# First and last stage of a three-block network kernel: the order of the loads, and the last columns by pairs

## The chip, the cores and the metric

The kernel runs on one core of a Trainium2 chip. The core has five engines with an instruction stream each: TensorE (matmuls and transposes, results in PSUM), VectorE, ScalarE, GpSimd and SyncE (SP), which only issues DMAs here. They are ordered among each other by semaphores alone. The metric is the device time of one execution in microseconds; lower is better. All data are fp32, and a product is made of three passes on high and low parts.

## What is computed

A sequence of 1024 positions with 1024 features goes through three blocks. Cut to what this change touches, the reference is:

```python
def rmsnorm(x, g):
    y = x * rsqrt(mean(x * x, -1) + EPS)
    return y * g

# first block, start
h = rmsnorm(x, norm_mix_g)
z = h @ w_in                      # the gate's low-rank columns (1536..) are projected first
q, k, v, g, a_f, a_b, su, sv = split(z)
...
# third block, end
pe = p @ w_pp                     # K = 256
gate = sigmoid(rms_norm_3(h, pe_norm_g) @ w_pg)
h = h + gate * pe
return rms_norm_3(h, final_g)
```

Between them lie gated linear attention and a spatial gating unit, an MLP, a state space layer with differential attention, and a convolution beside a gated recurrence.

## The kernel before

The program of every engine is written as functions of its own (`pe_...`, `act_...`, `dve_...`, `pool_...`, `sp_...`), called in program order. A table `at` gives every event a semaphore and a count: `inc` records it and `wait_ge(*at[event])` waits for it. `ended` and `fence` record and await the end of a stage on all semaphores. DMAs of SP rotate over 16 semaphores and those of ScalarE over 8, and `Engine.dma` waits until the earlier DMA on the same semaphore has landed.

Activations stand transposed in `HTh` and `HTl` (high and low part, features on partitions, 8 groups of 128 = k, two halves of 512 positions = th). Weights come in units: up to 8 x 128 rows by 256 columns, loaded by SP into one of three `WR` buffers (`sp_unit`), copied by ScalarE to a rounded high part in one of two `WH` buffers (`act_unit`), subtracted by VectorE to a low part in one of three `WL` buffers (`dve_unit`), and used by TensorE (`pe_unit`, `pe_done`). In the first call `sp_unit` takes units 0 to 2, `act_unit` and `dve_unit` take units 0 and 1; each later call takes one more, so the splits run one unit ahead of TensorE. Unit 0 has 128 columns (512 KB), unit 1 and most others 256 (1 MB); a `w_pp` unit has two groups of 128 rows only (256 KB).

PSUM has eight banks of 128x512: the ring `PD` with four for the projections and the ring `PB` with four (the two halves of the two `PQt` tiles). `take` goes round a ring; some users take fixed banks with `put`: squares go to `PB` banks 0 and 1, the late transposes to 2 and 3, and attention writes to `PQt` directly.

**Setup.** GpSimd makes the identity and zeroes four tiles `PRc`. SP loads four groups of small vectors (`COLS`; 10, 1, 1 and 9 parts) as rows into them, and four lambda vectors. TensorE transposes each tile, VectorE copies it to `PC` (so `pc(name, i)` is a column with one value per partition) and makes the lambda values, with one exponential by ScalarE between. Then all engines pass a fence.

**First norm and projection.** SP loads x in 8 tiles (`sp_load_x`). ScalarE squares each with an accumulator (`act_squares`, L484), VectorE and GpSimd make 1/sqrt per half (L492, L497), VectorE scales (L562), TensorE transposes (`pe_to_ht`, L359), ScalarE and VectorE write high and low part with the norm's gain (L523, L531). `act_norm` and `dve_norm` call `between` (the unit split, L311 and L320) after the first half's splits. TensorE's order is: transposes of half 0, projection `fm` of unit 0 for half 0 (L211, 24 matmuls), the late transposes of half 1 in two `PB` banks, `fm` for half 1, then the filling rounds.

**The end.** `pe_final` goes over four groups of 256 output columns (n) and in each over four pairs of tiles (t4): gate products `pg` from a `w_pg` unit, then `pp` products from a `w_pp` unit; a pair takes 48 matmuls for `pg` and 12 for `pp`. ScalarE writes the sigmoid (L3768), VectorE multiplies it by `pp` (L3782), GpSimd adds it to `X3` (L3795). After n = 3 ScalarE squares the eight tiles (L484), the powers are made per half (L492, L497), VectorE scales by half (L1583), and SP stores each tile.

Of the kernel before, what the change touches and what calls it, by code (L numbers as in the profile page):

```python
# [17 lines left out]
NT = 8  # L18
# [209 lines left out]
def program(nc, A, out, ctx):  # L228
# [74 lines left out]
    def act_unit(e):  # L303
        n = turn("act")
        for i in ([0, 1] if n == 0 else [n + 1]):
            if i < len(units):
                e.wait_ge(*at["w_landed", i])
                if i >= 2:
                    e.wait_ge(*at["w_used", i - 2])
                z = units[i][0]  # L310
                e.activation(WH[i % 2][:, 0:z], WR[i % 3][:, 0:z], ACT.Copy).then_inc(*at.inc("wh", "wh", i))  # L311

    def dve_unit(e):
        n = turn("dve")
        for i in ([0, 1] if n == 0 else [n + 1]):
            if i < len(units):
                z = units[i][0]
                e.wait_ge(*at["w_landed", i])
                e.wait_ge(*at["wh", i])
                e.tensor_tensor(WL[i % 3][:, 0:z], WR[i % 3][:, 0:z], WH[i % 2][:, 0:z].bitcast(F32),  # L320
                                SUB).then_inc(*at.inc("wl", "wl", i))

    def sp_unit(e):
        n = turn("sp")
        for i in ([0, 1, 2] if n == 0 else [n + 2]):
            if i < len(units):
                if i >= 3:
                    e.wait_ge(*at["w_used", i - 3])
                for dst, src in units[i][1]:
                    e.i.dma_start(dst, src).then_inc(*at.landed(f"wr{i % 3}", "w_landed", i))  # L330
# [69 lines left out]

    ph = ExitStack()
    PRc = [sbt(ph, [128, 128]) for _ in COLS]
# [4 lines left out]
    def pool_setup(e):  # L407
        e.memset(ident[:, :], 0.0).then_inc(*at.inc("pool", "z"))
# [6 lines left out]
        for i in range(4):  # L415
            e.memset(PRc[i][:, :], 0.0).then_inc(*at.inc("pool", "PR0", i))

    def sp_setup(e):
        for i, parts in enumerate(COLS):
            e.wait_ge(*at["PR0", i])  # L420
            for j, (name, ap) in enumerate(parts):
                r = col[name] - i * 128
                e.dma(PRc[i][r:r + ap.shape[0], :], ap, "col_in", i, j)
        for i, n in enumerate(("lambda_q1_2", "lambda_k1_2", "lambda_q2_2", "lambda_k2_2")):
            e.dma(lv[:, i, :], A[n].partition_broadcast(128).rearrange("p a d -> p (a d)"), "lv", i)

    def pe_setup(e):
        e.wait_ge(*at["const"])
        for i, parts in enumerate(COLS):
            b = e.take(PB, "col", i)  # L430
            for j in range(len(parts)):
                e.wait_ge(*at["col_in", i, j])
            e.transpose(b[:, 0:128], PRc[i][:, :], ident[:, :]).then_inc(*at.inc("pe", "col", i))

    def dve_setup(e):
        for i in range(4):
            e.wait_ge(*at["col", i])
            e.tensor_copy(PC[:, i * 128:i * 128 + 128], PB.of("col", i)[:, 0:128]).then_inc(
                *at.inc("dve", "PC", i, free=("col", i)))
        for i in range(2):  # L440
# [5 lines left out]
            e.tensor_reduce(lam[:, i:i + 1], lv[:, 4, :], AX.X, ADD).then_inc(*at.inc("dve", "lvs", i))  # L446
        e.wait_ge(*at["lam_exp"])
# [3 lines left out]
        e.wait_ge(*at["PC", 0])  # L451
        e.tensor_scalar(pc("subln"), pc("subln"), 1.0 - LAM_INIT, None, MUL).then_inc(*at.inc("dve", "subln"))

    def act_setup(e):
        e.wait_ge(*at["lvs", 1])
        e.activation(lam[:, 0:2], lam[:, 0:2], ACT.Exp).then_inc(*at.inc("act", "lam_exp"))
# [6 lines left out]
    def sp_load_x(e, X, src, *event):  # L463
        v = src.rearrange("(t p) d -> p t d", p=128)
        for tt in range(NT):
# [90 lines left out]
    def dve_norm(e, X, XN, v, ready, gname, vacant=(), between=lambda e: None):  # L556
# [9 lines left out]
        for tt in range(4):  # L566
            scaled(tt)
# [3433 lines left out]
```

## Time and profile before

| | |
|---|---|
| median of three timed runs | 3949.09 us (3943.42, 3949.09, 3951.37) |
| the profiled execution | 3947.51 us |
| its span | 3945.6 us |
| TensorE busy | 3713.4 us, 94% |
| VectorE / ScalarE / GpSimd busy | 2167.5 / 1653.1 / 520.3 us |
| TensorE's mean granted clock | 0.973 of 2.4 GHz |

Engines run beside each other, so busy times don't add up to the span. What counts is the time in which TensorE has nothing to do, and why. Times in the rows are microseconds from the start of the span; PEclk is the share of 2.4 GHz that was granted.

### The profile page before, as it was taken

How to read it: one execution, taken by the hardware profiler on the slowest of the kernel's cores; microseconds unless marked ns; L12 is line 12 of the kernel's file. 1: busy time of each engine (PE TensorE's matmuls, PEld its weight loads, DVE VectorE, ACT ScalarE, POOL GpSimd, SP SyncE). 2: the span in 40 equal slices, each digit the busy share in tenths (PEclk: the TensorE clock that was granted, in tenths of full speed). 3: DMA queues.
4: the chain of work that ended last, by engine and by line, in shares of the span. 5: the costliest groups of instructions: out<-in, count | busy, mean ns of one | idle time of the engine just before them, and what ended most of it. 6: DMA issues, size and time to landing. Idle time of an engine off the chain costs nothing.

```text
span 3945.6 us, 48879 instructions
## 1 busy us (share of the span) xinstructions
PE 3713.4 (94%) x20470; PEld 3102.4 (79%) x20470; DVE 2167.5 (55%) x2859; ACT 1653.1 (42%) x2267; POOL 520.3 (13%) x437
## 2 busy tenths in 40 slices
PE   6979999999999899989999998989999999989998
PEld 5758988877787677777777777978877778778998
DVE  4343344334446566645665655358888877853332
ACT  4322232121113555646776674144555545542132
POOL 0000010010001243510000000012222221210001
PEclk9989999999999899999999999999999999999999
DMA  3101211111111111010111114121111111143111
GB/s 95 33 11 50 75 59 54 43 51 46 43 54 55 43 33 43 12 49 24 33 35 27 35 48 163 49 75 43 43 43 38 49 48 38 38 183 132 44 44 59
DMA packets 196399, 211.32 MB, mean 54 GB/s; under 512 B 7943, under 2 KB 171732, under 8 KB 196180
## 3 DMA queue, kind: packets, MB, share of 16 engines
q1 hardware_dynamic: 191572, 191.42, 15.3%
q10 hardware_dynamic: 4608, 16.78, 1.1%
q8 instruction: 162, 2.65, 0.3%
q14 instruction: 57, 0.47, 0.0%
HBM read 174.62 MB, written 33.55 MB: 53 GB/s over the span
## 4 chain that ended last, share of the span: by engine, by line
PE 78%; DVE 9%; ACT 6%; issue 4%; DMA 1%; POOL 1%; SPq 0%; DVEq 0%; ACTq 0%; POOLq 0%
PE pd L211 66%; PE pq L211 9%; PE pd L359 2%; PE pq L359 1%; ACT t L311 1%; DVE t L320 1%; DVE t L2989 1%; ACT t L2586 1%; DVE t L3426 1%; ACT t L523 1%; DVE t L2981 0%; DVE t L1923 0%; DVE t L1495 0%; DVE t L3411 0%; DVE t L531 0%
## 5 line engine op out<-in xcount | busy, mean ns | idle before, releaser
L211 PE MATMUL pd<-t 128*128 128x512 f32 (+2 forms) x15920 | 3080.9, 354 | 41.6 <-DVE t L1495 10.1
L211 PEld LDWEIGHTS pd<-t 128*128 128x128 f32 x15920 | 2556.5, 191 | 513.0 <-issue 90.2
L211 PE MATMUL pq<-t 128*128 128x128 f32 (+5 forms) x3222 | 542.8, 331 | 83.6 <-DVE t L3465 21.5
L211 PEld LDWEIGHTS pq<-t 128*128 128x128 f32 (+2 forms) x3222 | 391.6, 182 | 184.4 <-issue 47.3
L311 ACT ACTIVATE t<-t 128x2048 fp32r<-128x2048 f32 (+2 forms) x150 | 244.9, 1633 | 677.9 <-PE pd L211 634.0
L320 DVE TENSOR_TENSOR t<-t 128x2048 fp32r<-128x2048 f32 (+2 forms) x150 | 297.3, 1983 | 287.8 <-ACT t L311 287.4
L1495 DVE TENSOR_TENSOR t<-pd,t 128x512 f32<-128x512 f32 x256 | 171.2, 689 | 115.7 <-PE pd L211 115.7
L1486 DVE TENSOR_TENSOR t<-t 128x512 fp32r<-128x512 f32 x64 | 45.8, 719 | 261.3 <-POOL t L1474 261.3
L3378 POOL TENSOR_TENSOR t<-t 128x512 f32<-128x512 f32 x56 | 89.8, 1603 | 616.8 <-ACT t L3322 608.9
L2989 DVE SCALAR_TENSOR_TENSOR t<-t 128x1024 f32<-128x1024 f32 x120 | 169.6, 1413 | 0.5
L2981 DVE SCALAR_TENSOR_TENSOR t<-t 128x1024 f32<-128x1024 f32 x120 | 166.2, 1385 | 1.7
L2709 DVE COPY t<-pd 128x512 f32<-128x512 f32 x64 | 44.3, 691 | 217.6 <-PE pd L359 217.6
L359 PE MATMUL pd<-t 128*128 128x128 f32 x800 | 119.8, 294 | 42.5 <-DVE t L562 18.6
L359 PEld LDWEIGHTS pd<-t 128*128 128x128 f32 x800 | 101.1, 152 | 65.2 <-issue 20.9
L2586 ACT ACTIVATE t<-t 128x1024 f32<-128x1024 f32 x128 | 145.8, 1142 | 13.8 <-DVE t L2663 13.8
L2658 DVE CUSTOM_DVE_ANT_0 t<-pq,t 128x1024 f32<-128x1024 f32 x128 | 151.2, 1219 | 0.0
L3322 ACT ACTIVATE t<-t 128x1024 f32<-128x1024 f32 x56 | 59.4, 1062 | 215.4 <-DVE t L3413 215.4
L1474 POOL TENSOR_TENSOR t<-t 128x512 f32<-128x512 f32 x64 | 68.2, 1067 | 613.1 <-ACT t L1424 613.1
L1424 ACT ACTIVATE t<-pd 128x512 f32<-128x512 f32 x64 | 38.3, 598 | 244.9 <-PE pd L211 244.9
L3426 DVE COPY_PREDICATED t<-t,pq 128x512 f32<-128x512 int32 x128 | 94.7, 743 | 70.1 <-PE pq L211 69.7
L1591 POOL TENSOR_TENSOR t<-t 128x2 f32<-128x2 f32 x8 | 10.4, 1303 | 917.5 <-DVE t L2826 857.1
L713 DVE TENSOR_TENSOR t<-pd,t 128x512 f32<-128x512 f32 x48 | 33.2, 691 | 176.5 <-PE pd L211 176.5
(295 smaller groups left out, 2830.5 us busy)
## 6 DMA issues: line engine op xcount, KB each, us to landing
t<-in_w_in_dram SPq DMA_DIRECT2D x97, 512.0 KB, 4.3
t<-in_w_mlp_dram SPq DMA_DIRECT2D x32, 1024.0 KB, 5.3
t<-in_w_out_dram SPq DMA_DIRECT2D x20, 1024.0 KB, 5.1
t<-in_w_in_dram SPq DMA_DIRECT2D x16, 1024.0 KB, 5.2
t<-in_x_dram SPq DMA_DIRECT2D x16, 512.0 KB, 6.6
x_scratch<-t SPq DMA_DIRECT2D x16, 512.0 KB, 2.6
ym_scratch<-t SPq DMA_DIRECT2D x16, 512.0 KB, 2.6
t<-x_scratch SPq DMA_DIRECT2D x16, 512.0 KB, 20.0
```

Source lines behind the costliest of these rows:

```text
L211: ins = e.matmul(out, l, r, start=(first and j == 0), stop=(last and j == n - 1), skip_group_check=True)
L311: e.activation(WH[i % 2][:, 0:z], WR[i % 3][:, 0:z], ACT.Copy).then_inc(*at.inc("wh", "wh", i))
L320: e.tensor_tensor(WL[i % 3][:, 0:z], WR[i % 3][:, 0:z], WH[i % 2][:, 0:z].bitcast(F32), SUB).then_inc(*at.inc("wl", "wl", i))
L359: ins = e.transpose(b[:, j * 128:(j + 1) * 128], s, ident[:, :])
L1474: e.tensor_tensor(q[:, :], r[:, :], r[:, :], MUL).then_inc(*at.inc("pool", "q", j, m, th, free=("r", j, m, th)))
L1495: e.tensor_tensor(X1[:, tt, half(nh)], PD.of("down", j, tt, nh)[:, :], X1[:, tt, half(nh)], ADD).then_inc(*at.inc("dve", "xadd", j, tt, nh ...
L2586: e.activation(s[:, r, :], s[:, r, :], ACT.Exp, bias=x[:, 2 + r:3 + r], accum_out=x[:, 4 + r:5 + r]).then_inc(*at.inc("act", "sexp", n))
L2658: e.tensor_tensor_reduce(out=s[:, r, :], in0=PQt[r][:, :], in1=bias[:, 896 - 128 * tt:896 - 128 * tt + 1024], scale=2.0 ** -(h + 1), scala ...
L2981: e.scalar_tensor_tensor(a[:, :], p[:, k:k + S], taps(k, g), a[:, :], MUL, ADD).then_inc(*at.inc("dve", "ctaps", g))
L2989: e.scalar_tensor_tensor(a[:, :], p[:, k:k + S], taps(k, g), a[:, :], MUL, ADD).then_inc(*at.inc("dve", "ctaps", g))
L3378: e.tensor_tensor(v4(z[:, :], w_)[:, :, 0, :], v4(k[:, :], w_)[:, :, 0, :], v4(dd[:, :], w_)[:, :, 0, :], MUL).then_inc(*at.inc("pool", "h ...
L3426: e.copy_predicated(At[:, th * 4:th * 4 + 4, :], bc(Mi[:, l:l + 1, :], [128, 4, 128]), four(PB.of("lv", h, l, th))).then_inc(*at.inc("dve" ...
```

## The change

At the start: x and the first normalised tiles get memory of their own ahead of the setup's. SP issues x tiles 0 to 3, unit 0, x tiles 4 to 7, and then the loads of small groups 1 to 3 and of the lambdas; ScalarE's queue issues those of group 0. The setup's fence is gone. TensorE transposes group 0 first and groups 1 to 3 after the second half of the first projection; VectorE copies group 0 first, and does the rest of the setup after the norm. The exponential of the lambdas stands after ScalarE's copies of the first projection. The first calls of the unit functions take one unit only, and `between` is called twice in the norm: between the halves' squares (ScalarE) or behind the first four scalings (VectorE), and after the first half's splits.

At the end, for the last columns (n = 3): the `pp` products come before the `pg` products and use `PB`; per pair of tiles VectorE multiplies and adds, ScalarE squares both tiles (output to SBUF), VectorE and GpSimd make 1/sqrt of the pair, and VectorE scales it behind the next pair's addition. The stores wait for tiles as before.

```diff
     def act_unit(e):
-        n = turn("act")
-        for i in ([0, 1] if n == 0 else [n + 1]):
-            if i < len(units):
+        i = turn("act")
+        if i < len(units):
...
     def sp_unit(e):
-        n = turn("sp")
-        for i in ([0, 1, 2] if n == 0 else [n + 2]):
-            if i < len(units):
+        i = turn("sp")
+        if i < len(units):
...
+    def act_setup(e):
+        e.wait_ge(*at["PR0", 0])
+        for j, (name, ap) in enumerate(COLS[0]):
+            r = col[name]
+            e.dma(PRc[0][r:r + ap.shape[0], :], ap, "col_in", 0, j)
+
     def sp_setup(e):
-        for i, parts in enumerate(COLS):
+        for i in range(1, 4):
...
     def pe_setup(e):
         e.wait_ge(*at["const"])
+        PB.put(2, ("col", 0))
+        pe_col(e, 0, PB.of("col", 0))
+
+    def pe_setup_rest(e):
+        for i in range(1, 4):
+            pe_col(e, i, e.take(PB, "col", i))
...
     def act_norm(e, X, v, ready, gname, between=lambda e: None):
-        for th in range(2):
-            act_squares(e, X, v, th, ready)
+        act_squares(e, X, v, 0, ready)
+        between(e)
+        act_squares(e, X, v, 1, ready)
...
         for tt in range(4):
             scaled(tt)
+        between(e)
         dve_rstd(e, v, 1)
...
         fm(e, u, 0, 1, 0, "a", 1)
         pe_done(u)
+        pe_setup_rest(e)
...
     def pe_final(e):
         for n in range(4):
+            if n == 3:
+                pe_embedded(e, n)
             u = pe_unit(e, A["w_pg_3"][0], [(n * 256, 256)])
...
             pe_done(u)
+            if n < 3:
+                pe_embedded(e, n)
+
+    def embedded(n, t4):
+        return (PB if n == 3 else PD).of("pp", n, t4)
...
     def act_final(e):
...
+                if n == 3:
+                    for tt in (2 * t4, 2 * t4 + 1):
+                        e.wait_ge(*at["padd_all"])
+                        e.wait_ge(*at["padd", 3, t4])
+                        e.wait_ge(*at.last("act"))
+                        e.activation(stage3[5 + tt % 3][:, :], X3[:, tt, :], ACT.Square,
+                                     accum_out=ss[:, 16 + tt:17 + tt]).then_inc(*at.inc("act", "fss", tt))
             act_unit(e)
-        for th in range(2):
-            act_squares(e, X3, "f3", th, lambda tt: ("padd", 3, tt // 2))
...
     def dve_final(e):
...
             for t4 in range(4):
+                gated(n, t4)
+                if n == 3:
+                    o = X3[:, 2 * t4:2 * t4 + 2, 768:1024]
+                    e.wait_ge(*at["gp", 3, t4])
+                    e.wait_ge(*at["padd_all"])
+                    e.tensor_tensor(o, o, two(gtr.of("gt", 3, t4)[:, :]), ADD).then_inc(
+                        *at.inc("dve", "padd", 3, t4, free=("gt", 3, t4)))
+                    if t4 == 0:
+                        e.wait_ge(*at["fg3"])
+                    else:
+                        scaled(t4 - 1)
+                    sl = slice(16 + 2 * t4, 18 + 2 * t4)
+                    e.wait_ge(*at["fss", 2 * t4 + 1])
+                    e.tensor_scalar(st[:, sl], ss[:, sl], 1.0 / 1024, 1e-6, MUL, ADD).then_inc(
+                        *at.inc("dve", "fms", t4))
+        scaled(3)
...
     def sp_program(e):
         own = ["wr0", "wr1", "wr2"] + [f"sp{i}" for i in range(RING["sp"])]
+        sp_load_x(e, X0, x_in, "x0", tts=range(4))
+        sp_unit(e)
+        sp_load_x(e, X0, x_in, "x0", tts=range(4, NT))
         sp_setup(e)
-        ended("setup", *own)
-        fence(e, "setup")
-        sp_load_x(e, X0, x_in, "x0")
         ended("norm", *own)
+        sp_unit(e)
         sp_unit(e)
```

## Rows read from the trace of the kernel before

**Rows 1.** The page, busy time of the engines, share of the span, instructions:

```profile
PE 3713.4 (94%) x20470; PEld 3102.4 (79%) x20470; DVE 2167.5 (55%) x2859; ACT 1653.1 (42%) x2267; POOL 520.3 (13%) x437
```

**Rows 2.** Busy time by stretch: stretch, length, engines' busy us, PEclk, DMA share, GB/s:

```profile
0.00:60.00 60.00, 24.35 (x102) 19.55 (x103) 22.68 (x39) 24.66 (x37) 4.93 (x17) 0.91 0.37 120
16.00:29.00 13.00, 0.00 (x0) 0.00 (x0) 2.52 (x6) 8.04 (x14) 1.02 (x1) 1.00 0.93 345
48.70:56.50 7.80, 4.85 (x32) 3.43 (x31) 4.23 (x6) 4.61 (x7) 0.00 (x0) 0.95 0.00 0
```

**Rows 3.** The chain that ended last, 0 to 72: start, us, what:

```profile
16.14 0.33 SPq L138
40.82 7.87 PE pd L211 x24
56.91 11.95 PE pd L211 x48
```

**Rows 4.** Timeline of the start: start, us, engine, line, operation, idle before:

```profile
0.81 1.28 ACT L456 ACT_TABLE_LOAD   x1 [0.81 <-PEq L3990]
1.94 0.40 SPq L138 DMA_DIRECT2D t<-in_norm_mix_g_dram  x1
5.05 0.25 SPq L138 DMA_DIRECT2D t<-in_subln_g_dram  x1
...
6.55 0.45 PE L433 MATMUL pq<-t 128*128 128x128 f32 x1 [6.55 <-DMA t<-in_ssm_norm_g_dram]
19.67 1.03 ACT L484 ACTIVATE pq<-t 128x1024 f32<-128x1024 f32 x1 [4.10 <-DMA t<-in_x_dram]
26.65 2.74 DVE L562 TENSOR_SCALAR t<-t 128x1024 f32<-128x1024 f32 x4 [1.23 <-POOL t L497]
29.14 1.03 ACT L484 ACTIVATE pq<-t 128x1024 f32<-128x1024 f32 x1 [0.19 <-DMA t<-in_x_dram]
29.54 6.43 PE L359 MATMUL pd<-t 128*128 128x128 f32 x32 [18.64 <-DVE t L562]
30.66 0.69 ACT L523 ACTIVATE t<-pd,t 128x512 fp32r<-128x512 f32 x1 [0.37 <-PE pd L359]
37.52 1.41 DVE L531 SCALAR_TENSOR_TENSOR t<-pd,t 128x512 fp32r<-128x512 f32 x2
65.98 2.29 DVE L320 TENSOR_TENSOR t<-t 128x2048 fp32r<-128x2048 f32 x1 [7.56 <-ACT t L311]
```

**Rows 5.** Prices: issues on ScalarE's queue, split, landing of w_pg, power (min/median/max):

```profile
3532.46 4.38 ACTq L138 DMA_DIRECT2D t<-zg_scratch  x8
...
L311 ACT ACTIVATE t<-t x2: 1057/1482/1907, 36.7 to 37.7; 128x1024 fp32r<-128x1024 f32 x1, 128x2048 fp32r<-128x2048 f32 x1
...
t<-in_w_pg_dram SPq DMA_DIRECT2D x3, 1024.0 KB, 5.1
...
L1591 POOL TENSOR_TENSOR t<-t x8: 695/1664/1672, 1229.6 to 2603.5; 128x2 f32<-128x2 f32 x8
```

**Rows 6.** Busy time by microsecond where the clock falls, columns as in rows 2:

```profile
38.00:39.00 1.00, 0.00 (x0) 0.00 (x0) 1.00 (x3) 1.00 (x1) 0.00 (x0) 0.79 0.00 0
...
55.00:56.00 1.00, 0.86 (x5) 0.63 (x6) 0.74 (x2) 0.16 (x1) 0.00 (x0) 0.82 0.00 0
```

**Rows 7.** Timeline of the end, columns as in rows 4:

```profile
3892.34 0.37 SPq L330 DMA_DIRECT2D t<-in_w_pp_dram  x1
...
3915.55 0.60 ACT L3768 ACTIVATE t<-pd 128x512 f32<-128x512 f32 x1 [5.16 <-PE pd L211]
3921.31 0.60 ACT L3768 ACTIVATE t<-pd 128x512 f32<-128x512 f32 x1 [5.16 <-PE pd L211]
...
3926.92 0.69 DVE L3782 TENSOR_TENSOR t<-pd,t 128x512 f32<-128x512 f32 x1 [0.72 <-PE pd L211]
...
3935.95 1.01 POOL L497 TENSOR_TENSOR t<-t 128x4 f32<-128x4 f32 x1 [5.07 <-DVE t L492]
3936.99 4.87 DVE L1583 SCALAR_TENSOR_TENSOR t<-t 128x1024 f32<-128x1024 f32 x4 [1.12 <-POOL t L497]
```

More of the change, by code:

```diff
@@ L399, in pc @@
         return PC[:, c:c + 1]
+    x_in = A["x"][0]
     ph = ExitStack()
+    X0 = sbt(ph, [128, NT, 1024])
+    XN0 = [sbt(ph, [128, 1024]) for _ in range(8)]
     PRc = [sbt(ph, [128, 128]) for _ in COLS]
@@ L450, in dve_setup, with sp_load_x @@
         e.tensor_scalar(lam[:, 3:4], lam[:, 2:3], -LAM_INIT, None, ADD).then_inc(*at.inc("dve", "lam"))
[L451 to L456, printed above, removed]
     ACT_OWN = ["act", "wh"] + [f"act{i}" for i in range(RING["act"])]
     DVE_OWN = ["dve", "wl"]
-    def sp_load_x(e, X, src, *event):
+    def sp_load_x(e, X, src, *event, tts=range(NT)):
         v = src.rearrange("(t p) d -> p t d", p=128)
-        for tt in range(NT):
+        for tt in tts:
             e.dma(X[:, tt, :], v[:, tt, :], *event, tt)
@@ L720, in units_only @@
             turns(e)
-    x_in = A["x"][0]
-    ph = ExitStack()
-    X0 = sbt(ph, [128, NT, 1024])
-    XN0 = [sbt(ph, [128, 1024]) for _ in range(8)]
-    ph.close()
     ph = ExitStack()
@@ L3796, in pool_final @@
                     *at.inc("pool", "padd", n, t4, free=("gt", n, t4)))
-        pool_rstd(e, "f3", 0)
-        pool_rstd(e, "f3", 1)
+        at.now("pool", "padd_all")
+        for p in range(4):
+            sl = slice(16 + 2 * p, 18 + 2 * p)
+            e.wait_ge(*at["fms", p])
+            e.tensor_tensor(st[:, sl], st[:, sl], nhalf[:, 0:2], ALU.pow).then_inc(*at.inc("pool", "frstd", p))
     def pe_program(e):
         pe_setup(e)
-        ended("setup", "pe")
-        fence(e, "setup")
         pe_stage_gla(e)
@@ L3820, in act_program @@
         act_setup(e)
-        ended("setup", *own)
-        fence(e, "setup")
         act_norm(e, X0, 0, lambda tt: ("x0", tt), "g_mix", between=act_unit)
@@ L3849, in dve_program @@
         own = DVE_OWN
-        dve_setup(e)
-        ended("setup", *own)
-        fence(e, "setup")
+        dve_col(e, 0)
         dve_norm(e, X0, [t[:, :] for t in XN0], 0, lambda tt: ("x0", tt), "g_mix", between=dve_unit)
@@ L3879, in pool_program @@
         pool_setup(e)
-        ended("setup", "pool")
-        fence(e, "setup")
         pool_norm(e, 0)
@@ L3910, in sp_program @@
         own = ["wr0", "wr1", "wr2"] + [f"sp{i}" for i in range(RING["sp"])]
+        sp_load_x(e, X0, x_in, "x0", tts=range(4))
+        sp_unit(e)
+        sp_load_x(e, X0, x_in, "x0", tts=range(4, NT))
         sp_setup(e)
-        ended("setup", *own)
-        fence(e, "setup")
-        sp_load_x(e, X0, x_in, "x0")
         ended("norm", *own)
+        sp_unit(e)
         sp_unit(e)
```

119 lines of the change are left out of this document (64 added, 55 removed).

## The prediction

> **What bounds the kernel now.** I read the page's busy shares first [rows 1]: TensorE is busy for 94% of the span, so most of the kernel is matmul time that the change leaves alone. Only places where TensorE waits can be worth anything. There are two at the edges that the diff touches. The table by stretches [rows 2] says that in the first 60 us TensorE is busy for 24.35 us, and the timeline of the end [rows 7] has all its work done by 3926.9, 18.7 us before the span is over.
>
> Next the chain of work that ended last [rows 3]. In the start it goes through the issues and the landing of the small loads, reaches the first issue of x at 16.14, waits for x, then goes through scaling, the transposes and splits, the first projection (40.82, 24 matmuls, 7.87 us), the late transposes, and the second half (56.91). From there TensorE is the chain. So everything before 56.9 is a chain of latencies, and a microsecond taken from it should be a microsecond of the end.
>
> The timeline of the start [rows 4] shows why x is late: SP issues the small loads from 1.94, and x from 16.14 only [rows 3], behind the setup's fence. The first square runs at 19.67, 3.5 us after the first issue of x. The eight squares are then nearly back to back (first start 19.67, last start 29.14, 1.24 us each), so ScalarE and the arrival of x go at about the same pace.
>
> At the end [rows 7], the last columns take TensorE 23 us of pg matmuls and then 5.8 us of pp matmuls; the last sigmoid is long done (3921.31) when the last pp product arrives (3926.92). After that come VectorE, GpSimd's additions, eight squares, two powers and eight scalings, down to 3936.99 + 4.87 = 3941.86, and the store.
>
> **The start, step by step.** (1) x is issued by SP without a wait. SP's queue is free at about 0.8 us (the const memsets are over by then, and ScalarE's first operation is at 0.81 [rows 4]), so I set the shift of x at 16.14 - 0.9 = 15.2 us. The first tile would land at 4.4, the fourth square could end at 25.12 - 15.2 = 9.9.
>
> (2) Ten loads of the first column group go to ScalarE's queue, in front of its squares. SP needed 3.36 us for the same ten (1.94 to 5.30 [rows 4]); eight large loads on ScalarE's queue took 4.38 us, 0.55 each [rows 5]. That bounds ten at 3.4 to 5.5 us; the ninth also waits until the first has landed, as that ring has 8 semaphores. With the table load of 1.28 us, before or behind them [rows 4], the first square starts between 5.7 and 8; I take 6.5, nearer to small loads. Four squares of 1.24 end at 11.5, 1.6 us later than x alone would allow.
>
> The Trainium skill (DMA: Bandwidth & Descriptors, Issuing engines are not separate DMA queues) says that loads of different engines run on the same 16 DMA engines and interleave, so that a second issuing engine saves only sequencer time. The trace has x alone filling them (0.93 from 16 to 29 [rows 2]), so it doesn't contradict this. By that rule the small loads share with x and land late; that is the first rival below.
>
> (3) The first weight unit is loaded behind the fourth x tile and split by ScalarE between the two groups of squares. Unit 0 is 512 KB, like a tile of x, which comes at 1.3 us per tile; with rows of 512 B I give it 1.3 to 2 us. It lands near 11, the split takes 1.06 [rows 5], 11.5 to 12.6, and four squares end at 17.6. The later x tiles land by about 16, so ScalarE is the chain. The splits of the transposed x start at 17.9 where they started at 30.66 [rows 4]: **12.8 us gained** of the 15.2.
>
> (4) VectorE: its first four scalings (2.74 us [rows 4]) run from about 13 to 15.7, its split of unit 0 (half of the 2.29 of a unit twice as large [rows 4]) to 17: both before ScalarE's first split, hidden. The interleaved splits and scalings keep their pace, and the last of the first half ends at 38.93 (37.52 + 1.41) - 12.8 = 26.1.
>
> (5) The projection. Before, TensorE had finished its transposes at 35.97 (29.54 + 6.43) and then stood until 40.82 for unit 0's split [rows 4, 3]. Now that split is long there. The matmuls can start at 35.97 - 12.8 = 23.2, with the last k at 26.1. Their duration depends on the granted clock: it fell from 2.4 to 1.2 GHz at 38.8 (a mean of 0.79 in that microsecond [rows 6]), after TensorE had been idle for about 3 us; it fell again at 55.8, after the late transposes with 4.85 us of work in 7.8 [rows 2, 6]. As before (7.87 us) they end at 31.1; at full clock (the 48 of the next group, partly slow as well, take 0.25 each [rows 3], so 24 at full clock some 5.5 us) at 28.7. I take 29.9, the middle, because the sparse transposes may bring the fall and the idle time that is removed may not. Before: 48.69. **18.8 us gained.**
>
> (6) The late transposes keep their 7.8 us, unit 1's split on VectorE (2.29 us, at 26.8 to 29.1) is hidden by the projection, and unit 1 itself: SP has 8 x loads and 15 small ones on 16 semaphores, so its last four small loads wait for x tiles 3 to 6 to land, and unit 1 is issued near 15 and lands by 21 (1 MB of weights: 5.1 us at the median [rows 5]); it is needed at 25.
>
> (7) The rest of setup now stands behind the norm. TensorE makes three transposes after the second half of the projection: 0.45 us for one alone before [rows 4], 0.7 for three that follow each other (between 0.4 and 1.35), so **0.7 us lost** on its own path. VectorE makes three copies and runs four small lambda operations, ScalarE waits for them ahead of unit 2's split. Both had room: VectorE stood 7.56 us before unit 2's split (65.98) [rows 4], and TensorE does 12 us of other matmuls (56.91, x48 [rows 3]) and then more of unit 1 before it needs unit 2. The cover is about 7 us for a delay of about 3 (my estimate from three copies, four operations and their hand-overs); without it 3 us would be lost. Sum of the start: 18.8 - 0.7 = **18.1 us**, with 14 to 21 as bounds (from the ends of (2), (3) and (5)).
>
> **The end, step by step.** Moving pp ahead of pg for the last columns keeps TensorE's work. The added wait: pg's last unit is now the very last, issued when pg of n=2 has been used (3892.3, the issue in [rows 7]); 1 MB lands in 5.1 us [rows 5], then ScalarE 1.91 [rows 5] and VectorE 2.29 [rows 4]; ScalarE also waits until pp of n=2 is through (3898.1): ready at 3902.4. TensorE has pp of n=2 and n=3 to do, each 48 matmuls like one pair of pg, which takes 5.76 us (3915.55 to 3921.31 [rows 7]): until 3903.9. Hidden, with 1.4 us to spare; below that spare it costs one for one.
>
> TensorE ends at 3926.9 as before. Then for the last pair: sigmoid 0.60, product 0.69, the addition, now on VectorE, 0.69, two squares of 1.2 (1.03 and the accumulator read; 1.24 from start to start [rows 4]), 0.17, the power, two scalings of 1.22 [rows 7]; VectorE's scalings of the pair before (2.43) lie beside the squares. The sum is 0.60 + 0.69 + 0.69 + 2.4 + 0.17 + 1.01 + 2.43 = 8.0, and half a microsecond for six hand-overs of about 0.08: 3935.4 instead of 3941.86. The power on two columns took 0.70 to 1.67 us elsewhere [rows 5]; I take the 1.01 of four columns at this place [rows 7] and keep both ends. Per pair ScalarE has 3.0 and VectorE 4.0 us of work in 5.76 us of matmuls, so earlier pairs don't pile up. The store's tail stays at 3.7 us (3941.86 to 3945.6). **6.4 us gained**, bounds 5 to 7.
>
> **Sum.** 18.1 + 6.4 = 24.5. The profiled execution took 3947.51 us (span 3945.6), 1.6 below the median of 3949.09, in a set that spreads over 8 us. 3947.5 - 24.5 = 3923.0 against its own time, 3924.6 against the median: I say 3924.
>
> **The rivals.**
> (A) Small loads late: they share the DMA engines with x, the ninth waits for the first, and squares start at 10 instead of 6.5. For: DMA is 0.93 busy under x. Against: they are few bytes; in the setup alone, TensorE's transpose ran at 6.55, 1.5 us after the tenth load's issue at 5.05 to 5.3 [rows 4]. The start loses 3.5 us more: 3928 (to 3931).
> (B) The clock falls during the transposes and stays low through the whole projection and again later: 24 matmuls at 0.43 us (512 columns at 1.2 GHz) instead of 0.33, and the pace of the transposes slows; 3 us: 3928 to 3930.
> (C) Everything warm and ScalarE free at once: 12.8 becomes 14, the projection 5.5 us: 3918.
> (D) The gain is lost in the middle: something after 60 us depends on an absolute time or on the state of rings: within 0.2%, about 3944.
> (E) Slower than before: setup takes three ring banks of PSUM instead of four, so every later use of the bank ring is moved by one against the users of fixed banks (squares on 0 and 1, late transposes on 2 and 3, at four later norms). If each such place had to wait for one more section of the kind that took 7.8 us [rows 2], 4 x 7.8 = 31 us would be lost and 24.5 gained: 3956. It decides from 24.5 us on, that is at four places of four. Against: all those places have long-free banks by their order in the code.
>
> **How the numbers follow.** Forecast (3920 to 3929) 0.55; C and better 0.13; A 0.15; B 0.08; D 0.06; E 0.03. The range 3914 to 3935 takes in A, B, C and the spread of the runs. About 0.2% (8 us) can be told from no change: faster 0.91, same 0.06, slower 0.03.
>
> **What would show it.** First square at 6 to 7; first split of x near 18; projection without a stop before it and its end near 30; from there the same order of work, shifted by 18; last VectorE scaling 8.5 us after TensorE's last matmul. Wrong would be: squares after 8, a stop of TensorE at about 3903 for the last weights, or stages between 60 and 3820 us that have changed their length by over 2 us.

## The result, and the profile after

The changed kernel took 3918.43 us (median of 4 runs, 3915.99 to 3919.33), the kernel before 3949.59 on the same chip (3943.42 to 3951.37): a ratio of 0.9923, with an interval of 0.9906 to 0.994. On a second chip it was 3917.02 against 3944.01, 0.9929 (0.9914 to 0.9944). The forecast was 3924, with a range of 3914 to 3935, and faster. The profiled execution took 3918.12 us with a span of 3916.2, so 29.4 us of span are gone, where the sum said 24.5.

The page of the kernel after, busy time of the engines, beside [rows 1]; then two stretches by the columns of [rows 2], the first 60 us and the late transposes:

```profile
PE 3705.7 (95%) x20470; PEld 3096.0 (79%) x20470; DVE 2170.6 (55%) x2865; ACT 1652.8 (42%) x2267; POOL 516.7 (13%) x435
```

```profile
0.00:60.00 60.00, 39.99 (x187) 31.49 (x188) 28.58 (x44) 32.90 (x46) 7.92 (x24) 1.00 0.43 138
29.30:36.80 7.50, 4.55 (x32) 3.13 (x31) 4.23 (x6) 4.33 (x7) 0.00 (x0) 1.00 0.00 0
```

TensorE does 39.99 us of work in the first 60 instead of 24.35, and its granted clock is 1.00 there (2.4 GHz throughout), where it was 0.91 [rows 2]. The late transposes are as sparse as before (4.55 us of work in 7.5), and this time the clock held.

The timeline of the start of the kernel after, which answers to [rows 3, 4]:

```profile
0.81 1.81 SPq L138 DMA_DIRECT2D t<-in_x_dram  x4
1.04 0.57 ACTq L138 DMA_DIRECT2D t<-in_norm_mix_g_dram  x1
5.89 0.23 ACTq L138 DMA_DIRECT2D t<-in_subln_g_dram  x1
6.15 1.28 ACT L503 ACT_TABLE_LOAD   x1 [6.15 <-DMA t<-in_norm_mlp_g_dram]
7.44 1.03 ACT L503 ACTIVATE pq<-t 128x1024 f32<-128x1024 f32 x1
10.42 0.45 PE L439 MATMUL pq<-t 128*128 128x128 f32 x1 [10.42 <-DMA t<-in_ssm_norm_g_dram]
12.22 1.04 ACT L310 ACTIVATE t<-t 128x1024 fp32r<-128x1024 f32 x1
17.93 1.28 ACT L542 ACTIVATE t<-pd,t 128x512 fp32r<-128x512 f32 x2
23.60 5.69 PE L211 MATMUL pd<-t 128*128 128x512 f32 x24 [0.87 <-ACT t L542]
36.81 5.72 PE L211 MATMUL pd<-t 128*128 128x512 f32 x24
42.37 0.49 PE L439 MATMUL pq<-t 128*128 128x128 f32 x3
48.26 1.98 PE L211 MATMUL pq<-t 32*128 32x512 f32 x4
```

x is issued from 0.81, the first square runs at 7.44, unit 0 is split at 12.22 between the squares, the splits of x start at 17.93, and the projection runs from 23.60 to 29.29, 0.24 us for a matmul. The four matmuls on 32 rows at 48.26, which I call the lambda projection, were at 68.79 in the trace of before: 20.5 us of shift, and I use them as the end of the start. The same place in the timeline of the kernel before:

```profile
56.56 12.30 PE L211 MATMUL pd<-t 128*128 128x512 f32 x48
68.79 1.98 PE L211 MATMUL pq<-t 32*128 32x512 f32 x4
```

The timeline of the end of the kernel after, which answers to [rows 7]:

```profile
3876.15 5.84 PE L211 MATMUL pq<-t 128*128 128x256 f32 x48
3876.41 1.92 ACT L310 ACTIVATE t<-t 128x2048 fp32r<-128x2048 f32 x1 [4.56 <-PE pd L211]
3878.43 2.29 DVE L318 TENSOR_TENSOR t<-t 128x2048 fp32r<-128x2048 f32 x1 [1.39 <-ACT t L310]
3881.83 23.19 PE L211 MATMUL pd<-t 128*128 128x256 f32 x192
3905.05 0.60 ACT L3790 ACTIVATE t<-pd 128x512 f32<-128x512 f32 x1 [1.27 <-PE pd L211]
3906.47 0.69 DVE L3824 TENSOR_TENSOR t<-t 128x512 f32<-128x512 f32 x1
3907.20 1.06 ACT L3797 ACTIVATE t<-t 128x1024 f32<-128x1024 f32 x1 [1.55 <-DVE t L3824]
3909.81 0.70 POOL L3847 TENSOR_TENSOR t<-t 128x2 f32<-128x2 f32 x1 [5.05 <-DVE t L3832]
3910.54 2.48 DVE L3812 SCALAR_TENSOR_TENSOR t<-t 128x1024 f32<-128x1024 f32 x2 [0.81 <-POOL t L3847]
```

The last pg unit is split by 3878.43 + 2.29 = 3880.72; TensorE comes out of pp at 3881.8 and goes on without a stop. Its last matmul ends at 3881.83 + 23.19 = 3905.02, the last scaling at 3913.02: a tail of 8.0 us, where it was 3941.86 - 3926.89 = 14.97. TensorE's last matmuls in the kernel before:

```profile
3916.73 10.15 PE L211 MATMUL pd<-t 128*128 128x256 f32 x84
```

The 29.4 us are: 20.5 in the start, 1.34 between the lambda projection and the last matmul (the shift grows from 20.53 to 3926.89 - 3905.02 = 21.87), 6.97 in the tail, and 0.56 in what follows the last scaling (3.18 instead of 3.74 us). The last of these isn't clear of chance: below, start_only with the old end has 3.43 there, and end_only with the changed end 3.57.

### The profile page after: what moved, and what is told of

The parts are those of the page before. It is cut to its first block, busy times and chain, and to the rows that moved or that the text cites. A ratio compares the mean times of both kernels' runs of the same rounds, so it can differ in the third digit from the quotient of the medians.

```text
span 3916.2 us, 48879 instructions
## 1 busy us (share of the span) xinstructions
PE 3705.7 (95%) x20470; PEld 3096.0 (79%) x20470; DVE 2170.6 (55%) x2865; ACT 1652.8 (42%) x2267; POOL 516.7 (13%) x435
## 3 DMA queue, kind: packets, MB, share of 16 engines
q8 instruction: 162, 2.65, 0.3%
## 4 chain that ended last, share of the span: by engine, by line
PE 78%; DVE 9%; ACT 6%; issue 5%; POOL 1%; DMA 1%; SPq 0%; DVEq 0%; ACTq 0%; POOLq 0%
PE pd L211 66%; PE pq L211 9%; PE pd L356 2%; PE pq L356 1%; ACT t L310 1%; DVE t L318 1%; DVE t L3004 1%; ACT t L2601 1%; DVE t L3441 1%; ACT t L542 1%; DVE t L2996 0%; DVE t L1938 0%; DVE t L1510 0%; DVE t L3426 0%; DVE t L1623 0%
## 5 line engine op out<-in xcount | busy, mean ns | idle before, releaser
L211 PE MATMUL pd<-t 128*128 128x512 f32 (+2 forms) x15872 | 3070.8, 354 | 37.5 <-DVE t L1510 10.1
```

What stands on the lines that cost most here:

```text
L211: ins = e.matmul(out, l, r, start=(first and j == 0), stop=(last and j == n - 1), skip_group_check=True)
```

## The experiments

**The two parts alone.** My theory was that the parts add up, the start with some 22 us (its middle counted in) and the end with 7.5. First the changed start with the old end: all hunks of the end are taken back, of which this is the core.

```
         for n in range(4):
-            if n == 3:
-                pe_embedded(e, n)
             u = pe_unit(e, A["w_pg_3"][0], [(n * 256, 256)])
...
-                if n == 3:
-                    for tt in (2 * t4, 2 * t4 + 1):
...
+        for th in range(2):
+            act_squares(e, X3, "f3", th, lambda tt: ("padd", 3, tt // 2))
```

> The changed start with the old end. Theory (the two ends are independent, each a chain of its own): TensorE's last matmul comes about 21.9 us earlier than in the profile of the kernel before, as in the changed kernel, and the tail after it stays at 15.0 us plus the store; the time is 3949.6 - 22 = 3927.5. Rival (the 1.2 us that the changed kernel gained between 60 and 3820 us is chance in the places where the clock falls, or belongs to the end): the shift at the last matmul is between 19 and 21, time 3929 to 3931.

Measured: 3927.47 us, ratio 0.9952 (0.9937 to 0.9967), span 3925.4. TensorE's last matmul ends at 3906.99 and the last scaling at 3921.97: the tail is 14.98 us, that of before, and the shift at the last matmul is 19.9. The time is that of the theory, but the shift is that of the rival (19 to 21, not 21.9): what the changed kernel had gained in the middle isn't there in this trace.

Then the old start with the changed end:

```
-        for i in range(1, 4):
+        for i in range(4):
             e.memset(PRc[i][:, :], 0.0)
...
-        between(e)
...
-        sp_load_x(e, X0, x_in, "x0", tts=range(4))
...
+        sp_load_x(e, X0, x_in, "x0")
```

> The old start with the changed end. Theory: from TensorE's last matmul to the last scaling 8.0 us instead of 15.0, and the store's tail about 3.2 instead of 3.7: 7.5 us, time 3942.1; nothing moves before 3820 us. Rival (moving pp ahead of pg costs TensorE something at the change of units): TensorE's last columns take more than the 29 us of before, and the gain is 5 to 6: 3944.

Measured: 3939.69 us, ratio 0.9982 (0.9972 to 0.9992), span 3935.6. The tail is 8.0 us (3924.03 to 3932.03). In medians the parts give 0.9952 x 0.9982 = 0.9934, inside the intervals of both measurements of the whole. So the places and sizes of the two gains hold. The profile of this run, however, showed a third thing. It was 2.4 us faster than the theory said, though the tail was as expected. Its start ended 1.1 us later than in the trace of before (69.86), but its last matmul came 2.9 us earlier (3924.03 against 3926.89), with 3750 us of instructions between that are the same. One step where the two part is from 1480 to 1500; the first line is of before, the second of this run (columns of [rows 2]):

```profile
1480.00:1500.00 20.00, 17.48 (x76) 13.43 (x75) 16.45 (x19) 14.33 (x27) 9.29 (x8) 0.91 0.00 0
```

```profile
1480.00:1500.00 20.00, 17.48 (x83) 13.61 (x82) 16.45 (x18) 13.82 (x27) 9.44 (x7) 1.00 0.00 0
```

TensorE is busy for 17.48 us in both, but in the second gets through 83 matmuls instead of 76, at a clock of 1.00 instead of 0.91.

**Both kernels once more,** without an edit, to see what belongs to one trace only.

> The kernel before once more, for a second trace. Theory (the stages between 60 and 3820 us differ by a few microseconds from execution to execution, by where TensorE's clock falls, so the 1.2 us that the changed kernel gained there are chance): against the first trace of the kernel before, the same instructions are moved by between -4 and +4 us at 3822, in steps where the clock falls. Rival (the middle is the same in each execution, and a change of it comes from the code): moved by under 0.3 us everywhere.

Measured: 3952.56 us, span 3950.7. The lambda projection was at 70.86, 2.1 us later than in the first trace, and the last matmul, at 3931.95, 5.1 later. Between them the distance went from 1.9 (at 2300) to 3.5 (2500), 0 (2800), 1.3 (3400), 3.7 (3800) and 5.1 (3900): the theory holds in size (3.7 at 3822, within its 4), and the rival of an unchanged middle is out.

```profile
70.86 1.98 PE L211 MATMUL pq<-t 32*128 32x512 f32 x4
3924.80 7.15 PE L211 MATMUL pd<-t 128*128 128x256 f32 x59
```

> The changed kernel once more, on another chip beside the kernel before, for its ratio and a second trace. Theory: start and end stand as in the first trace (second half of the projection at 36.8, or up to 2 us later where the clock falls after the late transposes; tail 8.0 us), the middle differs by up to 4 us; ratio 0.992 to 0.994. Rival: all within 0.3 us of the first trace.

Measured: 3917.02 us, ratio 0.9929 (0.9914 to 0.9944), span of the profile 3918.6. The tail is 8.0 again. The start is not the same: the first projection keeps the clock, the late transposes lose it. Timeline of the two halves, then two microseconds by the columns of [rows 2]:

```profile
23.42 5.71 PE L211 MATMUL pd<-t 128*128 128x512 f32 x24 [0.87 <-ACT t L542]
37.65 6.93 PE L211 MATMUL pd<-t 128*128 128x512 f32 x24
```

```profile
33.00:34.00 1.00, 0.65 (x3) 0.65 (x4) 0.95 (x2) 0.17 (x1) 0.00 (x0) 0.67 0.00 0
34.00:35.00 1.00, 1.00 (x7) 0.92 (x5) 0.00 (x0) 0.50 (x1) 0.00 (x0) 0.50 0.00 0
```

At 33 to 34 the clock goes from 1.00 to a mean of 0.67, then 0.50 (1.2 GHz) until 40, behind a stretch of transposes with gaps. The second half starts 0.8 us later and takes 1.2 us longer, and the lambda projection is at 50.32 instead of 48.26. So one pair of traces doesn't settle what the start gives: the three traces with the old start have the lambda projection at 68.79, 69.86 and 70.86 (mean 69.84), and the five with the start as changed (these two, start_only and the later pg_first and pool_add) between 48.26 and 50.32, with a mean of 49.33.

**Unit 0 split where it was.** Is it the early split that starts the projection and keeps the clock?

```
     act_squares(e, X, v, 0, ready)
-    between(e)
     act_squares(e, X, v, 1, ready)
...
                 between(e)
+                between(e)
```

The same in VectorE's norm.

> The changed kernel, but unit 0 is split where it was before, behind the splits of the first half of x. ScalarE's squares end 1.0 us earlier (16.8), so x's splits start near 16.9. Theory (the early split takes away a stop of TensorE, and with the stop the fall of its clock): TensorE stands from about 22 to 26.7 and then runs the 24 matmuls partly at 1.2 GHz in about 7.9 us, so they end near 34.5 instead of 29.3; 5 us are lost, up to 7 if the clock also falls after the late transposes: 3923.5 to 3925.5. Rival (the clock held by chance of phase, not for the missing stop): the stop costs itself, 26.7 + 5.7 = 32.4, and 3 us are lost: 3921.5.

Measured: 3925.99 us, ratio 0.9948 (0.9933 to 0.9963). The timeline of the projection, and the stretches before and in it:

```profile
27.71 8.01 PE L211 MATMUL pd<-t 128*128 128x512 f32 x24 [4.72 <-DVE t L318]
```

```profile
22.00:27.70 5.70, 0.99 (x7) 0.77 (x7) 5.70 (x9) 4.51 (x5) 0.00 (x0) 0.83 0.32 103
27.70:35.70 8.00, 7.99 (x26) 6.33 (x27) 2.11 (x1) 0.00 (x0) 0.00 (x0) 0.70 0.00 0
```

TensorE stands 4.72 us for VectorE's part of unit 0, the clock falls while it stands (0.83), and the projection takes 8.01 us at a mean clock of 0.70. It ends at 35.72 instead of 29.29: 6.4 us, 4.1 of them from the stop and 2.3 from the clock. Both expectations were too low, the rival's (a stop with no clock in it) by more. The nine traces of a changed start with the split where the change puts it have 5.69 to 5.72 us for these 24 matmuls (x_first, below, apart); all four with a stop of over 4 us in front of them have 7.87 to 8.29.

**The column group on SP's queue.** If ScalarE's ten issues cost its squares 3 us, SP should make them, behind the four tiles of x.

```
-    def act_setup(e):
+    def sp_cols(e):
...
-        act_setup(e)
...
         sp_load_x(e, X0, x_in, "x0", tts=range(4))
+        sp_cols(e)
         sp_unit(e)
```

> The changed kernel, but SP issues the ten small loads of group 0, behind x tiles 0 to 3 and ahead of unit 0; ScalarE's queue has none. Theory (the squares start late because ScalarE issues loads, waits for two semaphores of its ring of 8, and only then loads its table): the first square starts at 4.4 instead of 7.44, the fourth ends near 9.9, unit 0 then sets the pace (landing 10 to 11) and x's splits start 1 to 2 us earlier than 17.93: 3916.5 to 3917.5. Rival (the DMA engines are full of x and the small loads land late on any queue, now behind four tiles): the copy of group 0 comes after 12 and VectorE's first mean waits for it; nothing is gained, 3918.5 to 3920.

Measured: 3919.81 us, ratio 0.9933 (0.9918 to 0.9947), not to be told from the kernel after. ScalarE and the column group's transposition:

```profile
4.20 1.03 ACT L503 ACTIVATE pq<-t 128x1024 f32<-128x1024 f32 x1 [2.12 <-DMA t<-in_x_dram]
10.50 0.45 PE L439 MATMUL pq<-t 128*128 128x128 f32 x1 [10.50 <-DMA t<-in_ssm_norm_g_dram]
11.30 1.06 ACT L310 ACTIVATE t<-t 128x1024 fp32r<-128x1024 f32 x1 [1.16 <-DMA t<-in_w_in_dram]
16.76 1.03 ACT L503 ACTIVATE pq<-t 128x1024 f32<-128x1024 f32 x1 [0.48 <-DMA t<-in_x_dram]
17.82 3.56 ACT L542 ACTIVATE t<-pd,t 128x512 fp32r<-128x512 f32 x6
```

The first square is 3.2 us earlier, as expected, and nothing comes of it: ScalarE now waits 1.16 us for unit 0 and 0.48 for the last tile of x, and the splits of x start at 17.82 instead of 17.93. So ScalarE was not the only limit. The landing of x with unit 0 inside it was 0.1 us behind. (This edit also moves the issue of unit 0 from 2.65 to 6.53 and of the later x tiles behind it; the next run leaves them where they were, and finds the same limit.) The group itself is transposed at 10.50 from SP's queue and at 10.42 from ScalarE's. The Trainium skill (DMA: Bandwidth & Descriptors, Issuing engines are not separate DMA queues) says that transfers issued by different engines share the same DMA engines, so that only issue time is saved; these two rows agree.

**A ring of 16 for ScalarE's loads.** The ninth issue waits until the first load has landed. What does that cost?

```
-RING = {"sp": 16, "act": 8}
+RING = {"sp": 16, "act": 16}
```

> The changed kernel with 16 semaphores instead of 8 for ScalarE's DMAs. Theory (ScalarE's ninth and tenth issue wait until the first and second load have landed): the ten are issued by 4.7 instead of 6.12, the table load follows, and the first square starts near 6.0 instead of 7.44; x's last tile lands near 16, so the splits of x start 0.5 to 1 us earlier than 17.93. Rival (it is the descriptor queue behind x that holds the ninth issue): it still comes at 4.6 or later and the first square at 7.4.

Measured in one run: 3915.76 us, span 3914.0.

```profile
4.09 0.32 ACTq L138 DMA_DIRECT2D t<-in_ssm_norm_g_dram  x1
6.04 1.03 ACT L503 ACTIVATE pq<-t 128x1024 f32<-128x1024 f32 x1
16.60 1.03 ACT L503 ACTIVATE pq<-t 128x1024 f32<-128x1024 f32 x1 [0.46 <-DMA t<-in_x_dram]
```

The ninth goes out at 4.09 instead of 4.66 and the tenth at 4.44 instead of 5.89: the squares start 1.4 us earlier. Again the last tile of x takes that back (ScalarE waits 0.46 us for it), and the splits start at 17.65, 0.28 us earlier than in the kernel after, less than expected. The column group gains nothing by the earlier issue either:

```profile
10.27 0.45 PE L439 MATMUL pq<-t 128*128 128x128 f32 x1 [10.27 <-DMA t<-in_ssm_norm_g_dram]
```

Its last load is issued 1.45 us earlier, and the group is usable 0.15 us earlier.

**All of x ahead of the weights.** The landing of x paces the start; so x goes first, then unit 0, split by ScalarE behind its fourth x split. (The last pair of the end was scaled by tile in this kernel too.)

```
-        between(e)
...
+                if th == 0 and k == 3:
+                    between(e)
...
         sp_load_x(e, X0, x_in, "x0", tts=range(4))
-        sp_unit(e)
+        sp_cols(e)
         sp_load_x(e, X0, x_in, "x0", tts=range(4, NT))
+        sp_unit(e)
```

> The changed kernel with SP issuing x tiles 0 to 3, the ten small loads, x tiles 4 to 7 and then unit 0, which ScalarE and VectorE split behind the fourth split of x; and in the last pair each tile has its own mean and power. Theory (in the run with the small loads on SP the start was paced by the landing of x's last tile, with unit 0 ahead of it): the last tile lands 1 to 2 us earlier, x's splits start at 16.2 to 16.8 instead of 17.9, and the first projection ends 0.5 to 1.5 us earlier if unit 0 isn't late; the tail is 7.3 instead of 8.0 us. Together 1 to 2 us: 3916.5 to 3917.5, hardly to be told apart in the time. Rival (VectorE is full in this stretch, so one split more between its others delays the last ones): the projection ends no earlier, 0.7 us from the tail alone.

Measured: 3922.14 us, ratio 0.9941 (0.9925 to 0.9958).

```profile
15.76 1.03 ACT L503 ACTIVATE pq<-t 128x1024 f32<-128x1024 f32 x1 [0.21 <-DMA t<-in_x_dram]
24.48 7.35 PE L211 MATMUL pd<-t 128*128 128x512 f32 x24 [2.00 <-DVE t L550]
```

The last square is a microsecond earlier and the splits of x start at 17.47, but the projection starts at 24.48, 0.9 us later than in the kernel after, behind a stop of 2.0, and takes 7.35 us. The rival held: VectorE's splits of x (L550), which now have unit 0's among them, come late for the projection, and that costs more than the earlier x gives. By tile, the tail was 8.4 us, not shorter: two powers of one column took 1.39 us each.

**pp behind pg for the last columns too.** The prediction set the 3.0 and 4.0 us of work for a pair against 5.76 us of matmuls, but it gave no part of the tail's gain to the new order, and only said that pg's last unit stays hidden. Here the order is the old one and the work by pairs stays.

```
         for n in range(4):
-            if n == 3:
-                pe_embedded(e, n)
...
             pe_done(u)
-            if n < 3:
-                pe_embedded(e, n)
+            pe_embedded(e, n)
```

> The changed kernel, but in the last columns pp comes behind pg again (the work by pairs stays). Theory (moving pp is what lets the pairs overlap TensorE): the four products then come 1.4 us apart at the very end, ScalarE needs 2.4 us for the squares of a pair and VectorE 4.0 us for its work, so VectorE is the bound: product, addition and the four pairs' scalings end some 4 us later than in the changed kernel, 12 us after TensorE's last matmul instead of 8.0. Rival (the pairs alone bring it): the tail stays at 8 to 9 us.

Measured in one run: 3925.43 us, span 3923.5, the tail 3904.10 to 3920.32 = 16.2 us, more than the 15.0 of before and more than either expectation. VectorE's products of the second and third pair, ScalarE's sigmoid of the third, and the last scalings:

```profile
3904.31 0.69 DVE L3803 TENSOR_TENSOR t<-pq,t 128x512 f32<-128x512 f32 x1 [0.31 <-ACT t L3787]
3908.00 0.58 ACT L3787 ACTIVATE t<-pd 128x512 f32<-128x512 f32 x1
3908.68 0.69 DVE L3803 TENSOR_TENSOR t<-pq,t 128x512 f32<-128x512 f32 x1 [0.38 <-ACT t L3787]
3917.84 2.48 DVE L3809 SCALAR_TENSOR_TENSOR t<-t 128x1024 f32<-128x1024 f32 x2 [0.81 <-POOL t L3844]
```

The products are 4.37 us apart, though TensorE delivers pp of a pair every 1.46 us: the sigmoid of the next pair stands behind the squares of this one in ScalarE's order. One round of sigmoid, product, addition and two squares thus takes 4.37 us. With pg last, TensorE delivers a pair only every 5.76 us, and the round fits in between. So the two edits of the end belong together: pairs alone lose 1.2 us in this trace, and with the order turned they gain 7. The new order without the work by pairs was not run.

**GpSimd adds the last columns.** VectorE's addition could go back to GpSimd.

```
     def dve_final(e):
...
-                    e.tensor_tensor(o, o, two(gtr.of("gt", 3, t4)[:, :]), ADD).then_inc(
...
     def pool_final(e):
...
+            e.tensor_tensor(o, o, two(gtr.of("gt", 3, p)[:, :]), ADD).then_inc(
```

> The changed kernel with GpSimd doing the additions of the last columns, as before the change, instead of VectorE. Theory (the addition of the last pair lies on the chain behind TensorE's last matmul): 1.3 to 1.4 us instead of 0.69 and one hand-over more, so the tail is 8.7 instead of 8.0 us. Rival (VectorE's scalings of the pair before are the bound of the tail): they start 0.7 us earlier without the addition, and the tail stays at 8.0.

Measured in one run: 3916.9 us, span 3915.0, the tail 3901.71 to 3911.79 = 10.1 us instead of 8.0.

```profile
3903.53 3.47 DVE L3812 SCALAR_TENSOR_TENSOR t<-t 128x1024 f32<-128x1024 f32 x2
3903.69 2.23 POOL L3843 TENSOR_TENSOR t<-t 128x512 f32<-128x512 f32 x1 [0.37 <-DVE t L3806]
```

The addition took 2.23 us on GpSimd, where the twelve of the other columns take 1.29 to 1.74 (median 1.30) in the kernel after, and VectorE's two scalings beside it 3.47 instead of 2.48; the last pair's scalings in this run, with no addition beside them, took 2.48 again. So 1.5 us of the 2.1 are the addition, and 0.5 is ScalarE's last sigmoid, which started at 3902.24 behind the late squares of the pair before. The Trainium skill (SBUF — State Buffer, Who interferes with whom) has GpSimd share a pair of ports with VectorE, under an exclusive lock; the two rows agree with that in the main: in turn the three operations would take 3.8 us, side by side 2.5, and they took 3.47. The span is still 1.2 us shorter than that of the kernel after, since the middle of this trace is shorter (last matmul at 3901.71 instead of 3905.02, lambda projection at 48.34 and 48.26); the tail is what the edit moved.

**Keeping TensorE busy in the late transposes.** If the fall of the clock there costs the 1 to 2 us, matmuls between the transposes should win them. Twelve are added, whose results nobody reads. First each four took their own bank, then all the same:

```
+            if u is not None and k in (1, 3, 5):
+                w = e.take(PD, "warm", k)
+                for _ in range(4):
+                    e.matmul(w[:, :], u.h[:, 0, 0:128], HTh[:, 0, half(0)], start=True, stop=True,
+                             skip_group_check=True)
```

> The changed kernel with twelve more matmuls of 512 columns whose results nobody reads: four behind the late transposes of k = 1, 3 and 5 of the first norm, where TensorE waits about 0.9 us for splits. Theory (in four of five traces of the changed start the clock falls to 1.2 GHz in the late transposes, because TensorE does little there, and it costs 1 to 2 us there and in the second half of the projection): the granted clock stays at 2.4 GHz, the late transposes take at most 8.3 us from the first to the projection, the 24 matmuls of the second half take 5.7 us; against the traces with the fall 1 to 2 us are gained, ratio 0.9920 to 0.9930, the time itself moved less than can be told. Rival (the fall comes from the long wait before, not from the little work in this stretch): it falls all the same, and the twelve add 0.5 to 1 us.

Measured: 3920.59 us, ratio 0.994 (0.9927 to 0.9954).

```profile
39.26 5.74 PE L211 MATMUL pd<-t 128*128 128x512 f32 x24 [2.21 <-ACT t L1198]
```

The clock stayed at 1.00, but the second half started at 39.26 instead of 36.81 and waited 2.21 us for ScalarE: the ring of banks was three further on, so that this half had to take the bank of the first half before ScalarE had emptied it. With one bank, taken at k = 1 and kept:

```
-                w = e.take(PD, "warm", k)
+                if k == 1:
+                    PD_warm.append(e.take(PD, "warm"))
+                w = PD_warm[-1]
```

> The changed kernel with the same twelve unread matmuls in the late transposes, but all in one PSUM bank, so that the ring isn't moved on by three and the second half of the projection doesn't have to wait for the bank of the first (a wait of 2.2 us in the run before). Theory: the clock stays at 2.4 GHz through the whole start, as in that run; the second half of the projection starts at 36.8 to 37.1 and takes 5.7 us, so it ends near 42.6, as in the one trace of the changed kernel without the fall, and 1 to 2 us before those with it. The time is that of the changed kernel or up to 2 us less: ratio 0.9920 to 0.9930, and the spread from run to run isn't smaller, as the later stages keep theirs. Rival (unread matmuls cost as much as the fall): second half ends after 43.6, ratio 0.994.

Measured: 3917.34 us, ratio 0.9924 (0.991 to 0.9937), span of the profile 3912.9.

```profile
30.01 1.17 PE L541 MATMUL pd<-t 128*128 128x512 f32 x4
36.89 5.73 PE L211 MATMUL pd<-t 128*128 128x512 f32 x24
```

Four matmuls take 1.17 us, the second half starts at 36.89 and takes 5.73, and the clock was 1.00 throughout the start: the start is that of the kernel after in its best trace (lambda projection at 48.36). That the unread matmuls keep the fall away is not shown by this: two runs with them had no fall, but neither had two of the seven traces without them. In the time it can't be told from the kernel after (0.9923 and 0.9929). Nothing here beats that kernel by more than the measurement can tell.

## Why the prediction was right, step by step

**(1) to (3), x and the splits.** The measured time lies in the range, but below the 3920 to 3929 that had the chance of 0.55; the steps show what the forecast lacked. x was issued at 0.81 (0.9 forecast). The first square came at 7.44, late in the range of 5.7 to 8: of the 6.4 us behind ScalarE's first issue, 1.4 are the ninth and tenth waiting for the ring, which I had named but not priced (ring of 16). The splits of x started at 17.93, as said (17.9). That it came out so well is part luck: I took ScalarE as the chain and the landing of x as done by 16, and the two runs that freed ScalarE showed x's last tile 0.1 to 0.3 us behind. And the first square came 0.9 us later than the 6.5 that I took, while the path from it to the first split took 10.5 us instead of 11.4: two misses that cancel. (The squares of before were 1.35 us apart on average, not 1.24, which is their distance where none waits for x.)

**(4) and (5), the projection.** It started at 23.60 (23.2) and ended at 29.29 (29.9). Here I had put the middle between full and low clock; the mechanism was clear from [rows 6], where TensorE had been idle before the fall. With the idle time gone, the clock held in all nine such traces, 5.7 us; with it back (split_late) it fell, 8.0. x_first, with a stop of 2.0 us, took 7.35. The middle should have been the full-clock end, 0.6 us better.

**The start in all.** The lambda projection moved by 20.5 us where the steps said 18.1. Of the 2.4 us, 0.6 are the first projection and 0.35 the late transposes. The rest, some 1.5, is the second half with the three setup transposes: 36.81 to 48.26 is 11.45 us, 56.56 to 68.79 had been 12.23, and I had charged 0.7 on top. The transposes took 0.49 us, but the old stretch had been run partly at the low clock [rows 6], and I took its length over as it stood. So the mis-sized term is again TensorE's clock. By the means over several traces (69.84 and 49.33) the size is the same, 20.5, and by the kernel after's second trace (50.32) 18.5.

**(6) and (7), what was called hidden, was.** Unit 1 was issued at 15.43 (near 15). ScalarE's split of unit 2 was at 44.63 and VectorE's at 46.63, neither with TensorE behind it.

**The end.** No stop before pg's last unit, with 1.1 us to spare (1.4 forecast). The tail is 8.0 (8.5), a gain of 6.97 (6.4); 0.3 us of the difference is the power, which took 0.70 us for two columns where I used the 1.01 of four, and the rest is in the hand-overs, for which I had put half a microsecond. What the prediction lacked is that the gain hangs on the order (pg_first): it priced the turn of pp and pg as a wait hidden or not, not as what spaces the pairs.

**The middle** was forecast to keep its length and has 1.34 us less in this pair of traces. From the lambda projection to TensorE's last matmul the other twelve traces are between 4.8 us shorter and 3.0 us longer than the first trace of before, and end_only, whose middle isn't touched, is 3.9 shorter. So the sign of being wrong that I named, 2 us in the middle, could not tell anything from a pair of traces. On average the eleven changed starts have 3.1 us less there and the three old ones 0.3 less; with 6.9 us between the extremes of those three, it stays open whether the change has a part in it. That the clock differs is seen at one place (1480 to 1500), and in the timed executions: of the 13 of the kernel before that stood beside start_only, the shortest (3938.48 us) had a mean granted clock of 0.975 and the longest (3952.76) of 0.971. A clock lower by 0.004 over 3950 us is worth at most 16 us, by my estimate, and the two are 14 apart. That it explains all of the spread between the traces is argued, not shown. The forecast of 3924 was thus 5.6 us high: 4.9 of it in the profiled execution (3923.0 against 3918.12), namely 2.4 in the start, 0.6 each in the last pair and behind the last scaling, and 1.3 in the middle; the rest is how the medians stand to the profiles.

**The rivals.** A (small loads late) came true in its cause only: the first group was usable at 10.42, 3.9 us behind where the setup alone had its like [rows 4], but its users came later still. The wait for the first load was real and cost the squares 1.4 us (ring of 16), not 3.5. (The 0.93 of the DMA engines that I put down to x alone was nearly so: x is 4.2 of the 4.5 MB in that stretch.) B's fall in the projection did not come; in the late transposes it came in five of seven traces in which nothing was done against it, for 1 to 2 us, and what decides between the five and the two stays open. C gave 3918, which is what was measured, but by luck: it was right in the clock and not in ScalarE, and its own two terms, 1.2 us each, take the forecast to 3921.6 only. D and E fell: all changed starts have the moved ring, and none has a middle that is longer than in the first trace of before.

## What to carry to other kernels

A stop of TensorE ahead of dense matmuls should be priced twice, as the stop and as the lower clock behind it: here 4.1 and 2.3 us. When an engine is relieved and nothing comes of it, look for the wait that has appeared on the same engine: two limits here stood 0.1 us apart. Work by pairs at the end pays only if the producer hands over the pairs no faster than the round of work repeats (5.76 us against 4.37 here; at 1.46 it lost); the order of the producers decides that.

## What the runs showed of the hardware that I had not expected

- Traces with the same instructions over 3750 us differed there by up to 6.9 us (before_again and end_only), and over the same 20 us TensorE's clock was 0.91 in one and 1.00 in another. A difference of that size between single traces needs the timed runs beside it.
- Ten small loads beside four tiles of x were usable at 10.42 when ScalarE had issued the last at 5.89, at 10.27 when it had at 4.44, and at 10.50 when SP had at 6.24; with SP's and all of x ahead of unit 0 it was 11.46 (x_first). In the setup alone it had been 1.5 us behind the last issue [rows 4].
- GpSimd's power took 0.70 us on two columns here, 1.39 on one (x_first), and up to 1.67 on two elsewhere [rows 5]: its time didn't follow its size.
- Beside GpSimd's addition, VectorE's scalings took 1.4 times as long (3.47 against 2.48 us), and the addition itself 2.23 us instead of a median of 1.30.
